# Attention of a hybrid block on one core: two heads per step, in the two row halves of TensorE, with two filling products per step

## The reference

```python
def block_attention(q, k, v, scale, unit, decay=None):       # blocks of 128 queries, 256 tokens, 8 heads
    ...
    def one_block(args):
        ib, q_blk = args
        s = jnp.einsum('bqhd,bkhd->bhqk', q_blk, k, preferred_element_type=jnp.float32) * scale
        if decay_t is not None:
            dq = lax.dynamic_slice_in_dim(decay_t, ib * QBLOCK, QBLOCK, axis=2)
            s = s + dq[:, :, :, None] - decay_t[:, :, None, :]
        ...
        s = jnp.where(mask[None, None], s, NEG_INF)
        pr = jax.nn.softmax(s, axis=-1)
        return jnp.einsum('bhqk,bkhd->bqhd', pr.astype(v.dtype), v)

# mla: q and k are 64 wide plus a rotated part of 32; v is 64 wide; mask in chunks of 64 tokens
# fox: q, k, v are 64 wide; causal; the decay is a cumulative sum of log gates
```

## Time and profile before

| | us |
|---|---|
| median of 3 runs | 2145.02 (2143.17 to 2148.01) |
| the profiled execution | 2139.36 |
| its span | 2137.6 |
| attention of layer 0, from its first score matmul to the first gemm behind it | 142.38 to 300.23 |
| attention of layer 1, likewise | 770.35 to 928.18 |

### The profile page before, as it was taken

The page is one execution under the profiler, slowest core; times in us unless marked ns, Lnnn a source line. Parts: engine busy times, 40 slices in busy tenths (PEclk is TensorE's granted clock), DMA queues, the critical chain, the costliest instruction groups (busy, mean ns, idle before and its releaser), DMA issues.

```text
span 2137.6 us, 36606 instructions
## 1 busy us (share of the span) xinstructions
PE 1905.7 (89%) x12954; PEld 1743.0 (82%) x12954; DVE 900.2 (42%) x1959; ACT 970.9 (45%) x1439; POOL 1316.6 (62%) x451
## 2 busy tenths in 40 slices
PE   6868999999997878999999993599999989888997
PEld 5856789999997766799999982478888868678997
DVE  3576445322334576445323349431212246553223
ACT  5623445644555523555544554452322334255443
POOL 6743459898895833469988882634444434226885
PEclk9979999999998879999999986799999989998999
DMA  6432236565564522246655662423222223114553
GB/s 219 160 115 87 87 121 219 189 207 194 195 204 134 186 86 75 99 153 198 210 197 189 201 238 74 136 86 99 99 97 91 96 74 103 58 44 139 181 183 116
DMA packets 67872, 301.31 MB, mean 141 GB/s; under 512 B 7424, under 2 KB 9728, under 8 KB 67584
## 3 DMA queue, kind: packets, MB, share of 16 engines
q1 hardware_dynamic: 66240, 296.70, 41.8%
q10 hardware_dynamic: 1472, 2.43, 0.3%
HBM read 298.04 MB, written 1.05 MB: 140 GB/s over the span
## 4 chain that ended last, share of the span: by engine, by line
issue 34%; PE 31%; POOL 30%; DVE 2%; ACT 1%; POOLq 1%; DVEq 0%; ACTq 0%
POOL wlo L727 30%; PE bank L761 10%; PE bank L764 9%; PE bank L765 9%; DVE bank L1975 0%; ACT bank L1383 0%; PE bank L1064 0%; PE bank L1067 0%; PE bank L1068 0%; PE bank L1103 0%; POOLq L731 0%; ACT split_acts L1394 0%; ACTq L1392 0%; PE bank L1091 0%; DVE split_acts L1511 0%
## 5 line engine op out<-in xcount | busy, mean ns | idle before, releaser
L727 POOL TENSOR_TENSOR wlo<-raw,whi 128x1280 fp32r<-128x1280 f32 x447 | 1316.4, 2960 | 801.5 <-ACT whi L1137 799.6
L761 PE MATMUL bank<-split_acts,whi 128*128 128x256 f32 (+1 forms) x3556 | 1102.7, 310 | 87.9 <-DVE split_acts L1511 51.6
L764 PE MATMUL bank<-split_acts,whi 128*128 128x256 f32 (+1 forms) x3556 | 1085.3, 305 | 0.0
L765 PE MATMUL bank<-split_acts,wlo 128*128 128x256 f32 (+1 forms) x3556 | 1084.3, 305 | 0.0
L761 PEld LDWEIGHTS bank<-split_acts,whi 128*128 128x128 f32 x3556 | 697.1, 196 | 139.1 <-issue 63.1
L1137 ACT ACTIVATE whi<-raw 128x1280 fp32r<-128x1280 f32 x447 | 563.1, 1267 | 398.7 <-PE bank L761 341.4
L764 PEld LDWEIGHTS bank<-split_acts,whi 128*128 128x128 f32 x3556 | 698.5, 196 | 22.7 <-issue 0.2
L765 PEld LDWEIGHTS bank<-split_acts,wlo 128*128 128x128 f32 x3556 | 697.8, 196 | 23.4
L2007 DVE SCALAR_TENSOR_TENSOR acts<-bank,acts 128x256 f32<-128x256 f32 x120 | 54.1, 481 | 223.1 <-PE bank L765 223.1
L773 PE MATMUL bank<-whi,split_acts 128*128 128x256 f32 x384 | 108.5, 315 | 40.7 <-POOL wlo L727 38.1
L2021 DVE TENSOR_SCALAR acts<-bank 128x512 f32<-128x512 f32 (+1 forms) x64 | 35.7, 558 | 204.3 <-PE bank L765 204.3
(11 more groups left out here) (226 smaller groups left out, 1662.9 us busy)
## 6 DMA issues: line engine op xcount, KB each, us to landing
raw<-in_stream SPq DMA_DIRECT2D x448, 640.0 KB, 3.8
acts<-in_x SPq DMA_DIRECT2D x1, 1024.0 KB, 6.0
acts<-in_ctx ACTq DMA_DIRECT2D x1, 1024.0 KB, 6.3
out<-acts SPq DMA_DIRECT2D x8, 128.0 KB, 2.0
acts<-in_const ACTq DMA_DIRECT2D x1, 832.0 KB, 9.3
acts<-in_const SPq DMA_DIRECT2D x1, 774.0 KB, 8.5
acts<-in_p ACTq DMA_DIRECT2D x2, 256.0 KB, 3.1
acts<-in_par SPq DMA_DIRECT2D x1, 86.0 KB, 2.0
```

The lines of the kernel that those rows point to most:

```text
L727: nc.gpsimd.tensor_tensor(wlo[slot][:, :], raw[slot][:, :], whi[slot][:, :].bitcast(F32), ALU.subtract).then_inc(lo_ready, 1)
L761: first = nc.tensor.matmul(out_ap, w_hi, hi_act(k), start=(k == 0), stop=False)
L764: nc.tensor.matmul(out_ap, w_hi, lo_act(k), start=False, stop=False)
L765: last = nc.tensor.matmul(out_ap, w_lo, hi_act(k), start=False, stop=(k == k_tiles - 1))
```

## The change

A step now takes one query block of both heads of a pair, so a sweep has 8 steps instead of 16 units. In `scores` the two heads' matmuls alternate between rows 0-63 (into one bank) and rows 64-127 (into another); in `values` they alternate between the output's columns 0-63 and 64-127. `turn` transposes both heads' probabilities, and one ACT instruction moves both. Each step has two filling tiles, in the same order as before. DVE does both logits, then both normalisations. The other DVE blocks: the two `lru_core` stand in steps 0 and 1, behind the normalisations of units 1 and 3 as before, but ahead of two tiles instead of one; the ratio, the series and the decay stand in steps 3, 4 and 5, each one tile later in the order than before. The decay mask now holds both heads of a pair in one tile, so that there are 4 of them per sweep and not 8.

```diff
...
-    onehot = np.zeros((P, 8), np.float32)
+    onehot = np.zeros((P, 4), np.float32)
...
-        onehot[base:base + 8] = np.eye(8)
+        onehot[base:base + 8] = np.eye(8)[:, base // 64::2]
...
-        rinv = stat[:, 6:7]
+        rinv = [stat[:, 6:7], stat[:, 7:8]]
...
-                def scores(kind, u):
-
-                    U = (0 if kind == "mla" else 16) + u
-                    h, qb = u // 2, u % 2
-                    r, nk = 64 * (h % 2), P * (qb + 1)
-                    rows, q_cols = slice(r, r + 64), slice(qb * P, (qb + 1) * P)
-
-                    pe.wait_ge(lg_done, lay * UNITS + U + 1)
-                    o = s_bank[u % 2][:, 0:nk]
+                def step_no(kind, i):
+                    return (0 if kind == "mla" else 8) + i
+
+                def scores(kind, i):
+
+                    I, m, qb = step_no(kind, i), i // 2, i % 2
+                    nk, q_cols = P * (qb + 1), slice(qb * P, (qb + 1) * P)
+
+                    pe.wait_ge(lg_done, lay * UNITS + 2 * I + 2)
                     if kind == "mla":
-                        if u == 0:
+                        if i == 0:
                             pe.wait_ge(mla_ready, lay + 1)
-                        nc.tensor.matmul(o, tile(qn, h // 2)[rows, q_cols], tile(kn, h // 2)[rows, 0:nk],
-                                         start=True, stop=False)
-                        last = nc.tensor.matmul(o, tile(qr, h // 4)[rows, q_cols],
-                                                tile(krm, (h // 2) % 2)[rows, 0:nk], start=False, stop=True)
+                        q_a, k_a = tile(qn, m), tile(kn, m)
+                        q_b, k_b = tile(qr, m // 2), tile(krm, m % 2)
                     else:
-                        if u == 0:
+                        if i == 0:
                             out_of_bank(("fk", 3))
                             pe.wait_ge(decay_ready, lay + 1)
                         if qb == 0:
-                            pe.wait_ge(lh_ready, lay * HEADS + h + 1)
-                        nc.tensor.matmul(o, tile(fq, h // 2)[rows, q_cols], tile(fk, h // 2)[rows, 0:nk],
-                                         start=True, stop=False)
-                        last = nc.tensor.matmul(o, tile(lh, h % 2)[rows, q_cols], rk[rows, 0:nk],
-                                                start=False, stop=True)
-                    last.then_inc(s_done, 1)
-
-                def turn(kind, u):
-
-                    U = (0 if kind == "mla" else 16) + u
-                    pe.wait_ge(p_done, lay * UNITS + U + 1)
-                    pe.wait_ge(pt_done, lay * UNITS + U + 1)
-                    for kb in range(u % 2 + 1):
-                        last = nc.tensor.transpose(t_bank[:, kb * P:(kb + 1) * P],
-                                                   tile(pr, u % 2)[:, kb * P:(kb + 1) * P], ident)
+                            pe.wait_ge(lh_ready, lay * 4 + m + 1)
+                        q_a, k_a = tile(fq, m), tile(fk, m)
+                        q_b, k_b = tile(lh, m % 2), rk
+                    for side in range(2):
+                        r = slice(64 * side, 64 * side + 64)
+                        nc.tensor.matmul(s_bank[side][:, 0:nk], q_a[r, q_cols], k_a[r, 0:nk], start=True, stop=False)
+                    for side in range(2):
+                        r = slice(64 * side, 64 * side + 64)
+                        nc.tensor.matmul(s_bank[side][:, 0:nk], q_b[r, q_cols], k_b[r, 0:nk], start=False, stop=True)\
+                            .then_inc(s_done, 1)
+
+                def turn(kind, i):
+
+                    I = step_no(kind, i)
+                    pe.wait_ge(pt_done, lay * STEPS + I + 1)
+                    for side in range(2):
+                        pe.wait_ge(p_done, lay * UNITS + 2 * I + side + 1)
+                        for kb in range(i % 2 + 1):
+                            c = side * 256 + kb * P
+                            last = nc.tensor.transpose(t_bank[:, c:c + P], pr[:, c:c + P], ident)
                     last.then_inc(t_done, 1)
 
-                def values(kind, u):
-                    U = (0 if kind == "mla" else 16) + u
-                    h, qb = u // 2, u % 2
-                    pair = U // 4
-                    if u % 4 == 0:
+                def values(kind, i):
+                    I, m, qb = step_no(kind, i), i // 2, i % 2
+                    pair = I // 2
+                    if qb == 0:
 
                         pe.wait_ge(o_out, lay * PAIRS + pair + 1)
-                    pe.wait_ge(pt_done, lay * UNITS + U + 2)
+                    pe.wait_ge(pt_done, lay * STEPS + I + 2)
                     v = vm if kind == "mla" else vf
-                    r = 64 * (h % 2)
                     cols = (pair % 2) * 256 + qb * P
                     for kb in range(qb + 1):
-                        last = nc.tensor.matmul(o_bank[r:r + 64, cols:cols + P],
-                                                v[:, kb * 512 + h * 64:kb * 512 + (h + 1) * 64],
-                                                tile(pt, u % 2)[:, kb * P:(kb + 1) * P],
-                                                start=(kb == 0), stop=(kb == qb))
+                        for side in range(2):
+                            h = 2 * m + side
+                            c = side * 256 + kb * P
+                            last = nc.tensor.matmul(o_bank[64 * side:64 * side + 64, cols:cols + P],
+                                                    v[:, kb * 512 + h * 64:kb * 512 + (h + 1) * 64], pt[:, c:c + P],
+                                                    start=(kb == 0), stop=(kb == qb))
                     last.then_inc(pv_done, 1)
 
...
                 for kind, fill in (("mla", MLA_FILL), ("fox", FOX_FILL)):
-                    for i in range(17):
+                    for i in range(9):
                         if i:
                             turn(kind, i - 1)
-                        if i < 16:
+                        if i < 8:
                             scores(kind, i)
-                            gemm(fill[i])
+                            gemm(fill[2 * i])
+                            gemm(fill[2 * i + 1])
                         if i:
                             values(kind, i - 1)
...
-                def move_turned(kind, u):
-                    U = (0 if kind == "mla" else 16) + u
-                    act.wait_ge(t_done, lay * UNITS + U + 1)
-                    act.wait_ge(pv_done, lay * UNITS + U + 1)
-                    nk = P * (u % 2 + 1)
-                    sc.activation(tile(pt, u % 2)[:, 0:nk], t_bank[:, 0:nk], ACT.Copy).then_inc(pt_done, 1)
+                def move_turned(kind, i):
+                    I = (0 if kind == "mla" else 8) + i
+                    act.wait_ge(t_done, lay * STEPS + I + 1)
+                    act.wait_ge(pv_done, lay * STEPS + I + 1)
+                    nk = P * (i % 2 + 1)
+                    both = [a[:, 0:512].rearrange("p (s n) -> p s n", s=2)[:, :, 0:nk] for a in (pt, t_bank)]
+                    sc.activation(both[0], both[1], ACT.Copy).then_inc(pt_done, 1)
...
-                    for i in range(17):
+                    for i in range(9):
                         if i:
                             move_turned(kind, i - 1)
-                        if i < 16:
-                            exp(kind, i)
...
                                 sc.activation(f_den, f_ab, ACT.Exp, scale=-1.0).then_inc(fl_exp, 1)
-                            keep_ahead(fill[i])
-                            of_tile(fill[i])
-                        if i and i % 4 == 0:
-                            attended(kind, (i - 1) // 4 + (0 if kind == "mla" else 4))
-
-                act.wait_ge(pv_done, lay * UNITS + UNITS + 2)
+                            for t in fill[2 * i:2 * i + 2]:
+                                keep_ahead(t)
+                                of_tile(t)
+                        if i and i % 2 == 0:
+                            attended(kind, i // 2 - 1 + (0 if kind == "mla" else 4))
...
-                    for i in range(17):
-                        if i < 16:
-                            logits(kind, i)
-                            normalise(kind, i)
-                        if kind == "mla" and i in (1, 3):
-                            lru_core(2 if i == 1 else 3)
-                        if kind == "mla" and i in (3, 5):
-                            lru_lo_part(2 if i == 3 else 3)
-                        if i < 16:
-                            of_tile(fill[i])
-
-                        if kind == "mla" and i == 6:
+                    for i in range(9):
+                        if i < 8:
+                            for u in (2 * i, 2 * i + 1):
+                                logits(kind, u)
+                            for u in (2 * i, 2 * i + 1):
+                                normalise(kind, u)
+                        if kind == "mla" and i in (0, 1):
+                            lru_core(i + 2)
```

(51 more changed lines are left out.)

17 lines of the change are left out of this document (10 added, 7 removed).

## The result

| | time, us | ratio to before |
|---|---|---|
| before, median of 4 runs beside it | 2145.94 | |
| changed, median of 4 runs (2077.04 to 2084.67) | 2082.01 | 0.9705 [0.9694, 0.9717] |
| forecast | 2102.6 (range 2088 to 2120) | 0.980 |

The change gains 63.9 us where 42.4 were forecast. The profiled execution of the changed kernel took 2084.67 us (span 2082.9), 54.7 less than that of before, and its two attention stretches are 29.4 and 29.6 us shorter; the rest of the program is 4 us longer. The windows answer to the earlier trace rows: mla and fox of layer 0, then of layer 1 (window, length, busy time of PE, its weight loads, DVE, ACT, POOL, then clock, DMA share, GB/s).

The account below looks back on a forecast made before the run. In the attention stretches PE's work and waits, not the weight stream, were taken to bound the kernel. Savings of 16.8 + 6 + 19.6 = 42.4 us from 2139.36 gave 2097.0, plus 5.66 to the median: 2102.6 us, range 2088 to 2120.

Parts of the forecast that it names:

- Term 1: PE's own order in attention: two heads per step without overlap take 5.85 us against 6.90, saving 16.8 us.
- Term 2: Both array halves working at once in scores and values: 6 us saved, 5.6 in fox and 0.4 in mla.
- Term 3: PE's waits and half clock in both sweeps: 13.4 us per layer instead of 23.2, saving 19.6 us in both.
- Rival B: Full overlap in both sweeps, and DVE lumps fit behind two tiles: 64 us less, 2081; chance 0.13.
- Rival A: No overlap at all, and waits fall by only 5.5 us per layer: 27.8 us less, 2117; chance 0.24.
- C: Slower: one POOL instruction each blocks both scalings in every step; 20 us slower, 2165; chance 0.03.
- D: Halves disturb each other on PE, 0.09 us per change of half: 22 us less, 2123; chance 0.10.

Follow-up runs that it names:

- kernel with nothing together: Changed kernel with both heads' score products reading rows 0-63 and value products, issued by head, all writing columns 0-63, so no halves overlap; 2103.87 us, ratio 0.981.

## Why the prediction was wrong

**Term 1 was right.** The kernel with nothing together shows the groups as summed: values 1.02, scores 1.92. Only the four transposes are shorter, 0.59 for 0.70 us: 18.6 us instead of 16.8.

**Term 2 is the step that failed.** The forecast took 6 us, and called 22.6 the most there could be. Both numbers were too small. Its words "each matmul is two instructions in the same half that can't overlap each other, so of 8 instructions in pairs A A B B A A B B at best 3 are hidden" assume that PE keeps its order across the halves. It doesn't: 4 of 8 are hidden, in both orders that were run. On PE that is 0.85 + 0.44 us for scores and 0.43 + 0.21 for values, 1.93 us per pair and 31 us in all, of which 16.1 + 5.8 = 22 come through. To take half of the best case in fox and 0.4 us in mla was a discount without a row for it. The Trainium skill ("TensorEngine Tiling (Array Packing)", Key Properties), which the prediction weighed, says that different tiles run weight loads and matmuls in parallel; the trace agrees, 1.07 us for two heads where 1.06 stood for one.

**Term 3 came out in sum only without the overlap.** The kernel with nothing together gains 41.0 us, 18.6 of them term 1: 22 us less of waits and half clock, for 19.6. In the changed kernel 9 of the 31 us of overlap come back: PE's waits in the attention of layer 0 are 12.0 us, for 6.0 with nothing together, and nearly all of the growth is in mla. An estimate from the earlier trace rows: before holds 63.7 + 70.9 = 134.6 us of work per layer, the changed kernel 134.6 - 8 x 3.10 = 109.8, so 18.6 of its 128.4 us are waits and half clock, where the forecast had 13.4. The forecast named this effect; it made it too large against its own term 2 (all but 0.4 us of mla's share taken back) and too small in the waits themselves. Of the 20.6 us by which the forecast missed, about 16 stand in term 2 (22 for 6), 2 in term 1 and 2 here. The wait view has 7 waits, in fox only at its two ends; the longest is behind the series, with the second POOL stall that it counted. DVE is busy 60.5 us in mla of layer 0 and 62.2 in that of layer 1 where it was 56.4, with the same 149 instructions.

**The rivals.** Rival B gives the time (2081), by luck in its parts: the overlap is full, but the blocks do not fit behind two tiles, they cost 22 us. It was held at 0.13 because its second half looked unlikely, though its first half alone, 19 us of overlap with waits as forecast, gives 2145.0 - 16.8 - 19 - 19.6 = 2089.6, close to the range's low end. Rival A, nothing together, is the kernel of 2103.9, not 2117. C and D are refuted: the transposes do not wait in each step, and a change of half costs 7 to 14 ns, not 90. Two small slips of the sums bear on nothing: C's 62 us of waits and order are 16.8 + 46.4 = 63.2, and mla's 79.4 leaves in the 0.2 us that it says are off.

**Open.** Why mla of before loses more to the same blocks, 15.5 and 16.3 us for 11.6 and 12.7 (twice as many handovers from DVE to PE that a block can hit), is argued, not shown. No kernel was run in which POOL's splits stand elsewhere, though the second stall of the series and the waits of 2.5 us lie beside them. Where the 4 us outside attention went was not tested; they are as large as the spread between runs.

## What to carry over

Put work that uses only half of the array's rows or columns next to its counterpart in the other half, and price the pair as one; the order inside the group was free here. Before discounting an effect that could be whole or absent, forecast both as cases instead of a value between them. When PE gets faster, look for the engine whose in-order blocks it now meets: here moving or cutting them did not help, only less work on DVE did. When an edit changes nothing in the time, add up the waits at the ends of the stretch too: a cost and a gain can stand behind it.

## What the hardware showed unexpectedly

- Matmuls of the two halves start 7 ns apart (13 to 14 when one head's four stand first) and run side by side at full rate: 1.07 us together, 1.92 in one half. The overlap reaches at least four instructions ahead.
- It holds for row halves that write two banks and for column halves that write one: 0.59 us together, 1.02 in one half.
- A long wait can cost twice: behind the 4.2 us wait the granted clock is 0.50 (1.2 GHz), and the two tiles after it take 6.24 us instead of 4.50.
